# A fourth buffer for the high parts of the weights in a two-layer fp32 trunk

## What is computed

```python
def swiglu(h, w_gate, w_up, w_down):
    a = jnp.einsum('bsd,df->bsf', h, w_gate)
    b = jnp.einsum('bsd,df->bsf', h, w_up)
    return jnp.einsum('bsf,fd->bsd', jax.nn.silu(a) * b, w_down)

def moe_swiglu(h, router, w_gate, w_up, w_down):
    logits = jnp.einsum('bsd,de->bse', h, router).astype(jnp.float32)
    vals, idx = lax.top_k(logits, TOP_K)
    gates = jax.nn.softmax(vals, axis=-1)
    combine = jnp.sum(jax.nn.one_hot(idx, N_EXPERTS, dtype=jnp.float32) * gates[..., None], axis=-2)
    y = jnp.zeros_like(h)
    for e in range(N_EXPERTS):
        y = y + combine[..., e:e + 1].astype(h.dtype) * swiglu(h, w_gate[e], w_up[e], w_down[e])
    return y

# trunk, for each layer i (D_FF = 3584)
#   h = h + mixer(rmsnorm(h, norm_mix[i]), ...)
#   h = h + (swiglu if i % 2 == 0 else moe_swiglu)(rmsnorm(h, norm_ffn[i]), ...)
```

## Time and profile before

| | |
|---|---|
| three runs | 1437.06, 1436.88, 1436.52 us, median 1436.88 |
| the profiled execution | 1437.3 us, span 1435.5 us |
| PE busy (matmuls) | 1386.6 us, 97% |
| DVE busy | 1125.5 us, 78% |
| ACT busy | 966.8 us, 67% |
| granted TensorE clock, mean | 0.998 |
| memory read | 431.60 MB, 301 GB/s over the span |

### The profile page before, as it was taken

The page is one execution under the profiler, slowest core; times in us unless marked ns, Lnnn a source line. Parts: engine busy times, 40 slices in busy tenths (PEclk is TensorE's granted clock), DMA queues, the critical chain, the costliest instruction groups (busy, mean ns, idle before and its releaser), DMA issues.

```text
span 1435.5 us, 18808 instructions
## 1 busy us (share of the span) xinstructions
PE 1386.6 (97%) x6673; PEld 1089.5 (76%) x6673; DVE 1125.5 (78%) x970; ACT 966.8 (67%) x904; POOL 13.7 (1%) x26
## 2 busy tenths in 40 slices
PE   9999999999999999999999999999999999999996
PEld 7888888888788787777787777778777778777774
DVE  6575544544656699999998899998999999999997
ACT  6555434344545578788777777887788777777876
POOL 1100000000000000000000000000000000000000
PEclk9999999999999999999999999999999999999999
DMA  9813555555450099999999999999999999999993
GB/s 357 306 58 132 205 177 192 187 177 194 157 174 2 17 385 395 395 393 393 400 354 348 394 393 392 394 382 337 380 387 393 394 399 350 358 388 393 394 396 147
DMA packets 184148, 433.19 MB, mean 302 GB/s; under 512 B 7066, under 2 KB 8265, under 8 KB 184112
## 3 DMA queue, kind: packets, MB, share of 16 engines
q1 hardware_dynamic: 182064, 426.80, 81.0%
q0 software_dynamic: 1888, 5.78, 1.3%
q10 hardware_dynamic: 160, 0.14, 0.0%
HBM read 431.60 MB, written 1.09 MB: 301 GB/s over the span
## 4 chain that ended last, share of the span: by engine, by line
PE 76%; DVE 11%; issue 8%; ACT 5%; DVEq 0%; ACTq 0%
PE ps L1419 19%; PE ps L1421 19%; PE ps L1420 19%; DVE wlo L878 9%; ACT whi L514 4%; PE ps L1853 3%; PE ps L1825 2%; PE ps L1826 2%; PE ps L1548 1%; PE ps L1750 1%; PE ps L1521 1%; PE ps L1426 1%; PE ps L1814 1%; PE ps L1815 1%; PE ps L1787 1%
## 5 line engine op out<-in xcount | busy, mean ns | idle before, releaser
L878 DVE TENSOR_TENSOR wlo<-raw,whi 128x2048 fp32r<-128x2048 f32 (+1 forms) x403 | 912.7, 2286 | 210.9 <-ACT whi L514 208.3
L514 ACT ACTIVATE whi<-raw 128x2048 fp32r<-128x2048 f32 (+1 forms) x403 | 766.8, 1913 | 221.5 <-PE ps L1421 207.7
L1419 PE MATMUL ps<-whi,xhi 128*128 128x512 f32 (+1 forms) x880 | 346.0, 393 | 4.9 <-DVE wlo L878 2.4
L1421 PE MATMUL ps<-whi,xlo 128*128 128x512 f32 (+1 forms) x880 | 342.3, 389 | 0.0
L1420 PE MATMUL ps<-wlo,xhi 128*128 128x512 f32 (+1 forms) x880 | 341.7, 388 | 0.0
L1419 PEld LDWEIGHTS ps<-whi,xhi 128*128 128x128 f32 x880 | 165.3, 188 | 42.3 <-DVE wlo L878 5.8
L1421 PEld LDWEIGHTS ps<-whi,xlo 128*128 128x128 f32 x880 | 165.2, 188 | 34.4
L1420 PEld LDWEIGHTS ps<-wlo,xhi 128*128 128x128 f32 x880 | 165.3, 188 | 32.6
L1814 PE MATMUL ps<-whi,xhi 128*128 128x512 f32 x392 | 159.2, 406 | 7.0 <-DVE wlo L878 4.8
L1815 PE MATMUL ps<-wlo,xhi 128*64 128x512 f32 x392 | 154.3, 394 | 0.0
L1419 PE MATMUL ps<-whi,thi 128*128 128x512 f32 x320 | 127.3, 398 | 0.0
(11 more groups left out here) (248 smaller groups left out, 1083.5 us busy)
## 6 DMA issues: line engine op xcount, KB each, us to landing
raw<-in_moe_up SPq DMA_DIRECT2D x112, 1024.0 KB, 8.2
raw<-in_moe_gate SPq DMA_DIRECT2D x112, 1024.0 KB, 8.4
raw<-in_moe_down SPq DMA_DIRECT2D x112, 1024.0 KB, 8.4
raw<-in_ffn_up SPq DMA_DIRECT2D x14, 1024.0 KB, 5.1
raw<-in_ffn_gate SPq DMA_DIRECT2D x14, 1024.0 KB, 5.1
raw<-in_ffn_down SPq DMA_DIRECT2D x14, 1024.0 KB, 4.8
raw<-in_dil_w_in SPq DMA_DIRECT2D x10, 1024.0 KB, 5.1
raw<-in_swa_w_in SPq DMA_DIRECT2D x4, 1024.0 KB, 17.8
```

Source lines behind the costliest of these rows:

```text
L514: act.activation(whi[:, c % CUT, 0:span(c)], raw[:, c % RAW, 0:span(c)], ACT.Copy).then_inc(hi_ready, 1)
L878: dve.tensor_tensor(wlo[:, c % CUT, 0:n], raw[:, c % RAW, 0:n], whi[:, c % CUT, 0:n].bitcast(F32), ALU.subtract).then_inc(lo_ready, 1)
L1419: pe.matmul(dst, ahi, bhi, start=start, stop=False)
L1421: return pe.matmul(dst, alo, bhi, start=False, stop=stop)
```

## The change

1. `whi` has four slots (`HIS = 4`), `wlo` still three (`LOS = 3`). ACT's cut waits for the unit four before. DVE's cut gets its own wait for PE, for the unit three before. PE reads `whi[:, c % HIS]` and `wlo[:, c % LOS]`.
2. To make room, `qk` and `probsT` (attention) get places that are later those of `xhi` and `xlo`, `yhi_b` and `ylo_b` (the small expert's result) the place of `memkv`, and `stats` shrinks from 304 to 272 columns.
3. Since 6 is no multiple of 4, the dense loop now has two steps in a turn on ACT, DVE and PE: three double turns on PE; two double turns and two steps written out behind the loop on ACT and DVE.
4. In `experts`, ACT and DVE have some small steps at another place among the cuts.

```diff
-CUT = 3
+HIS = 4
+LOS = 3
@@ tiles
-        whi = sb("whi", [P, CUT, UNIT], F32R)
-        wlo = sb("wlo", [P, CUT, UNIT], F32R)
+        whi = sb("whi", [P, HIS, UNIT], F32R)
+        wlo = sb("wlo", [P, LOS, UNIT], F32R)
...
-        memkv = sb("memkv", [P, 2, TILES, 512])
+        with ExitStack() as until_routing:
+            memkv = sb("memkv", [P, 2, TILES, 512], scope=until_routing)
+        yhi_b = sb("yhi_b", [P, D], F32R)
+        ylo_b = sb("ylo_b", [P, D], F32R)
@@ cut on ACT
-                wait(act, units_done, c + RAW * rounds - CUT + 1)
-                act.activation(whi[:, c % CUT, 0:span(c)], raw[:, c % RAW, 0:span(c)], ACT.Copy).then_inc(hi_ready, 1)
+                wait(act, units_done, c + RAW * rounds - HIS + 1)
+                act.activation(whi[:, c % HIS, 0:span(c)], raw[:, c % RAW, 0:span(c)], ACT.Copy).then_inc(hi_ready, 1)
@@ dense_step on ACT (DVE alike)
-            with act.Fori(1, STEPS - 1) as s:
-                dense_step(s)
-            dense_step(STEPS - 1, True)
+            with act.Fori(0, (STEPS - 2) // 2) as k:
+                for odd in (1, 0):
+                    dense_step(2 * k + (2 - odd), odd)
+            dense_step(STEPS - 2, 1)
+            dense_step(STEPS - 1, 0, True)
@@ cut on DVE
                 dve.wait_ge(hi_ready, c + RAW * rounds + 1)
+
+                wait(dve, units_done, c + RAW * rounds - LOS + 1)
                 n = span(c)
-                dve.tensor_tensor(wlo[:, c % CUT, 0:n], raw[:, c % RAW, 0:n], whi[:, c % CUT, 0:n].bitcast(F32),
+                dve.tensor_tensor(wlo[:, c % LOS, 0:n], raw[:, c % RAW, 0:n], whi[:, c % HIS, 0:n].bitcast(F32),
                                   ALU.subtract).then_inc(lo_ready, 1)
@@ dense loop on PE
-            with pe.Fori(1, STEPS) as s:
-                products_in(FFN0 - 2, s, TILES, s * TILES)
-                unit_out(FFN0 + 2, s, dense, 0)
-                for t in range(TILES):
-                    hidden_t(t, s * TILES + t)
-                unit_out(FFN0 + 3, s, dense, 1)
+            with pe.Fori(0, STEPS // 2) as k:
+                for odd in (1, 0):
+                    s, c, even = 2 * k + (2 - odd), FFN0 + 6 * odd, 2 * k + (2 - 2 * odd)
+                    products_in(c - 2, even, TILES, s * TILES)
+                    unit_out(c + 2, even, dense, 0)
+                    for t in range(TILES):
+                        hidden_t(t, s * TILES + t)
+                    unit_out(c + 3, even, dense, 1)
```

More of the change, by code:

```diff
@@ L208, in trunk @@
             ylo = sb("ylo", [P, D], F32R, scope=glu)
-            yhi_b = sb("yhi_b", [P, D], F32R, scope=glu)
-            ylo_b = sb("ylo_b", [P, D], F32R, scope=glu)
             zero = sb("zero", [P, 512], F32R, scope=glu)
@@ L679, in _, with dense_step @@
                 glu_thi(t, t, FFN0 + 4, turned(t)[0])
-            def dense_step(s, last=False):
+            def dense_step(s, odd, last=False):
                 for i in range(4):
-                    cut(FFN0 + i, s)
+                    cut(FFN0 + 6 * odd + i, s - odd)
                 glu_silu(0, s * TILES, g_done, s + 1, rstd[:, 4:5])
@@ L686, in dense_step @@
                 for i in range(2):
-                    cut(FFN0 + 4 + i, s)
+                    cut(FFN0 + 6 * odd + 4 + i, s - odd)
                 for t in range(TILES):
@@ L798, in experts @@
                         y_hi(1, b)
-                for i in range(3, 6):
+                for i in range(3, 7):
                     cut(MOE0 + i, r)
                 large_silu(pair, 0, pair_unit(pair, 3))
-                for i in range(6, 8):
+                for i in range(7, 9):
                     cut(MOE0 + i, r)
@@ L806, in experts @@
                 put_out(pair)
-                cut(MOE0 + 8, r)
+                cut(MOE0 + 9, r)
                 sums_of(1, pair_unit(pair, 7))
-                cut(MOE0 + 9, r)
                 with act.Fori(1, STEPS) as s:
@@ L1362, in experts @@
                     c, rs = MOE0 - 4, r + 2 * s
-                    for i in range(2):
+                    for i in range(3):
                         cut(c + i, rs)
                     small_mul(pair, s - 1)
-                    for i in range(2, 5):
+                    for i in range(3, 5):
                         cut(c + i, rs)
                     small_tlo(pair, s - 1)
-                    cut(c + 5, rs)
+                    for i in range(5, 7):
+                        cut(c + i, rs)
                     large_mul(pair, s)
-                    for i in range(6, 11):
+                    for i in range(7, 11):
                         cut(c + i, rs)
@@ L1376, in experts @@
                     build_pick(pair + 1)
-                for i in range(2):
+                for i in range(3):
                     cut(MOE0 + PAIR_UNITS - 4 + i, r)
                 small_mul(pair, STEPS - 1)
-                for i in range(2):
-                    cut(MOE0 + PAIR_UNITS - 2 + i, r)
+                cut(MOE0 + PAIR_UNITS - 1, r)
                 small_tlo(pair, STEPS - 1)
@@ L1475, in chunk @@
                         last = three(dst, xhi[:, kt, t * P:(t + 1) * P], xlo[:, kt, t * P:(t + 1) * P],
-                                     whi[:, u % CUT, cols], wlo[:, u % CUT, cols], kt == 0, kt == 4 * n_units - 1)
+                                     whi[:, u % HIS, cols], wlo[:, u % LOS, cols], kt == 0, kt == 4 * n_units - 1)
                     if t == TILES - 1:
@@ L1560, in in_tile @@
                     last = three(ps[:, bank[t], :], xhi[:, kt, rows_], xlo[:, kt, rows_],
-                                 whi[:, c % CUT, cols], wlo[:, c % CUT, cols], kt == 0, kt == KT - 1)
+                                 whi[:, c % HIS, cols], wlo[:, c % LOS, cols], kt == 0, kt == KT - 1)
                 return last
@@ L1580, in out_tile @@
                         cols = slice(j * D + b * 512, j * D + b * 512 + 512)
-                        last = three(ps[:, B_Y[t][b], :], hi[:, ft, :], lo[:, ft, :], whi[:, c % CUT, cols],
-                                     wlo[:, c % CUT, cols], False, final and half == 1 and j == 1)
+                        last = three(ps[:, B_Y[t][b], :], hi[:, ft, :], lo[:, ft, :], whi[:, c % HIS, cols],
+                                     wlo[:, c % LOS, cols], False, final and half == 1 and j == 1)
                 return last
@@ L1716, in _ @@
                         last = three(ps[:, chunk_bank(c, t), :], xhi[:, kt, t * P:(t + 1) * P],
-                                     xlo[:, kt, t * P:(t + 1) * P], whi[:, u % CUT, cols], wlo[:, u % CUT, cols],
+                                     xlo[:, kt, t * P:(t + 1) * P], whi[:, u % HIS, cols], wlo[:, u % LOS, cols],
                                      kt == 0, kt == 3)
@@ L1811, in small_in @@
                     both, own = xhi[:, kt, P:2 * P], xhi[:, kt, P:P + HALF]
-                    hi, lo = whi[:, c % CUT, cols], wlo[:, c % CUT, cols]
+                    hi, lo = whi[:, c % HIS, cols], wlo[:, c % LOS, cols]
                     if kt < KT - 1:
@@ L1824, in small_products @@
                 cols = slice(j * D + b * 512, j * D + b * 512 + 512)
-                pe.matmul(ps[0:HALF, B_Y[1][b], :], thi[:, ft, P:P + HALF], wlo[:, c % CUT, cols], start=False, stop=False)
-                return pe.matmul(ps[:, B_Y[1][b], :], thi[:, ft, P:2 * P], whi[:, c % CUT, cols], start=False, stop=stop)
+                pe.matmul(ps[0:HALF, B_Y[1][b], :], thi[:, ft, P:P + HALF], wlo[:, c % LOS, cols], start=False, stop=False)
+                return pe.matmul(ps[:, B_Y[1][b], :], thi[:, ft, P:2 * P], whi[:, c % HIS, cols], start=False, stop=stop)
             def small_out(c, rounds, half, final=False):
```

37 lines of the change are left out of this document (21 added, 16 removed).

## The result

The changed kernel takes 1415.84 us (median of four runs, 1414.31 to 1417.08) against 1436.82 us for the kernel before (four runs): 21.0 us less, a ratio of 0.985 with a 95% interval of 0.9837 to 0.9862. Forecast was 19.5 us less.

The account below looks back on a forecast made before the run. The prediction took buffers and the load queue's 394 GB/s ceiling to bound expert turns equally, at 31.9 us. Gains of 16.2 + 1.3 + 2.0 = 19.5 us gave 1417.4 us, range 1409 to 1427 us (80%).

Parts of the forecast that it names:

- The bound: Expert stage: three buffers bind the 31.90 us turn, and its 12 loads at 394 GB/s take the same 31.9 us.
- Rival A: Expert stage: 394 GB/s is no ceiling, all turns fall to 30.1 us, 46 to 50 us won; chance 4%.
- B: Changes of pair: six raw buffers, freed by DVE, alone set the queue's idle time; 0 to 10 us won; chance 11%.
- The changes of pair: Three passages between expert pairs: loads run ahead there, winning 5.4 of 7.9 us idle time each, 16.2 us.
- PE's own pace: Expert turns without the limit of loads: matmuls, fold, transposes and 0.2 for passages make 30.1 us a turn.
- The first pair: Six turns before 718 us, already at the loads' ceiling: only a lead of 1.7 us to give, 1.3 taken.
- The end: Last unit of the expert stage: rounded earlier with a buffer free, 2.0 us won, bounds 0 and 2.3.
- DVE's new wait: DVE's cuts: waiting for PE directly adds no time; a fulfilled second wait costs under 0.05 us.
- Rival C: Expert loop: two semaphore tests per cut make DVE the bound; at 0.3 us each +16 us, 1453 us; chance 5%.
- The doubled dense loop: Dense loop unrolled twice: PE branches over a longer body at no cost; upper end 5.1 us, twice.
- Rival D: Dense loop: the longer body stalls PE at its branches, 5.1 us at most twice, 1422 to 1428 us; chance 4%.
- The new places: Moved qk, probsT, yhi_b, ylo_b and smaller stats: addresses only, no instruction or wait, put at nothing.

Follow-up runs that it names:

- e5: Kernel before with every load of the expert stage halved to 512 KB: 1437.74 us, ratio 1.0004.
- e8: Changed kernel with one more load of 256 KB in each of the 24 inner turns: 1430.35 us.
- e10: Changed kernel with stats back at 304 columns, so thi lies 128 bytes behind a multiple of 4096: 1417.65 us, ratio 0.9859.
- e11: Changed kernel with stats at 288 columns, so thi lies 64 bytes behind a multiple of 4096: 1416.95 us, ratio 0.9854.
- e12: Changed kernel with gate (8 bytes per partition) allocated behind both_halves instead of ahead of it: 1414.31 us, ratio 0.984.
- e3: Changed kernel with three whi buffers and the old order of small steps in experts: 1434.18 us, ratio 0.9975.
- e9: Kernel before with stats at 272 columns instead of 304, nothing else: 1433.8 us, ratio 0.9969.
- e1: Changed kernel with experts on ACT and DVE in the old order of small steps, four whi buffers kept: 1424.75 us, ratio 0.991.
- e6: Changed kernel with every load of the expert stage halved to 512 KB: 1385.32 us, ratio 0.9635.
- e7: Kernel before with one more load of 256 KB in each of the 24 inner turns: 1440.59 us, ratio 1.0016.

## Why the prediction was right, point by point

**The bound: right.** Both halves hold. Buffers bound the kernel before (e5: 31.92 us a turn with half the loads), and the loads are a ceiling at nearly the same 31.9 (late turns of the changed kernel, 394 GB/s; e8 at 32.60 with 256 KB more, 394 GB/s again). Hence the gain is not 1.8 us in each turn. Rival A is out (its own terms add up to 50 to 51 us, not to the 46 to 50 that it names), and so is B, as the stretches of 224.77 to 227.34 us show.

**The changes of pair, 16.2 us: right, 16.5 measured**, but not evenly: 231.61 became 227.34, 231.26 became 225.57, 231.30 became 224.77, that is 4.3, 5.7 and 6.5 us instead of 5.4 each. Over the 223.6 us of a stretch's loads there remain 3.7, 2.0 and 1.2 us, on the mean 2.3, where 2.4 to 2.5 were forecast. They do not lie where the forecast put them. Behind the first change the queue moves 380 GB/s in the long turn and 368 in the turn behind it, which against 394 are about 1.4 and 2.0 us of idle time; the forecast had 1.8 and 0.6. The first change gives least in e10 and e11 too; what holds it back was not tried.

**PE's own pace: 30.1 forecast, 29.86 measured.** 0.17 of it is the place of thi and tlo (e10: 30.03), the rest the allowance for passages between matmuls, which was too large. The lead is gone in two turns, or three in the last pair, where three or four were forecast. The faster pace explains only a part of that, since 6.1 us of lead at 2.0 us a turn would last three turns. The other part is probably that the queue stands idle in the turn behind the change too, and so builds less lead.

**The first pair, 1.3 us: 3.2 measured, but the lead gave what was forecast.** The forecast let the shrinking lead give 1.7 us and took 1.3. The rest comes from loads that land earlier, which the forecast did not have. This shows when one and the same load, the 51st of the expert stage, is followed through the profiled executions, together with the mark that ends the first pair (us from the start of the span):

| | 51st load lands | first pair ends | earlier than before, beyond the load |
|---|---|---|---|
| kernel before | 630.08 | 718.29 | |
| changed kernel | 628.52 | 715.13 | 1.6 |
| e10 | 630.50 | 717.12 | 1.6 |
| e11 | 629.42 | 716.02 | 1.6 |
| e12 | 628.54 | 715.16 | 1.6 |

All four have the new buffer and order, and each ends the pair 1.6 us earlier than its loads alone would make it: this is the lead, close to the 1.7 us. The other 1.6 us of the changed kernel are its loads' earlier landing, and that changes with the place of the tiles: with stats at 272 columns (changed kernel, e12) the loads land 1.5 to 1.6 us earlier than before, with 304 or 288 columns (e10, e11) 0.4 later to 0.7 earlier. The time from issue to landing is no measure of the gain. It rose by 3.0 us, from 8.4 to 11.4, and it is 11.4 in e10 too, whose first pair ends only 1.2 us earlier than before.

**The end, 2.0: right, 2.1.**

**DVE's new wait, nothing: right.** Its cuts take 2.28 to 2.29 us as before, back to back they start 2.20 us apart as before, and e3, which has the wait, is within 0.4 us of e9, which has not. Rival C is out.

**The doubled dense loop, nothing: right.** The line of the loop's branch on PE in the changed kernel, against the earlier trace rows:

```profile
L1687 PEldq COMPARE_BRANCH  x3: 76/213/226, 221.7 to 355.9; - x3
```

Starts of matmuls in the loop are nowhere more than 0.33 us apart, so no turn stalls, and e3 with the doubled loop is as fast as e9 without. Rival D is out. The Trainium skill (Runtime: NRT & Kernel Launch, Instruction fetch mechanics) has a taken branch stall when its target is not in the window of pages; no such stall is seen here. Whether the target of this branch, 304 matmuls and as many weight loads back, lies outside that window no run shows, so the trace speaks against the stall here and not against the rule.

**The new places, "at nothing, because they are addresses only": wrong.** It is the one step that failed in kind. stats at 272 columns takes 3.7 us off the kernel before (e9), and one to three us of what the changed kernel gains are its doing (e10 to e12). It does not show in PE's sums: PE was 198.00 of 198.00 us busy at either distance, since a modelled duration of 0.39 us overlaps the next start 0.23 us later. The changed kernel shows the same full sum for the dense loop, 160 to 358 us:

```profile
sum 198.00, PE 198.00 PEld 164.43 DVE 99.25 ACT 83.17 POOL 0.00; mean PE 198.00 PEld 164.43 DVE 99.25 ACT 83.17 POOL 0.00
```

Mean durations on the page of the kernel before do show it, if one asks why the same shape takes 5 to 7 ns longer with another stationary operand:

```profile
L1419 PE MATMUL ps<-whi,xhi 128*128 128x512 f32 (+1 forms) x880 | 346.0, 393 | 4.9 <-DVE wlo L878 2.4
...
L1420 PE MATMUL ps<-wlo,xhi 128*128 128x512 f32 (+1 forms) x880 | 341.7, 388 | 0.0
...
L1419 PE MATMUL ps<-whi,thi 128*128 128x512 f32 x320 | 127.3, 398 | 0.0
...
L1420 PE MATMUL ps<-wlo,thi 128*128 128x512 f32 x320 | 126.3, 395 | 0.0
```

In the dense loop the shorter distance is worth 7 steps x 48 matmuls x 5.5 ns = 1.8 us, and the first load behind routing was issued at 498.58 us instead of 501.09. Over all profiled executions that load is issued at 498.5 to 500.0 us where stats has 272 columns (nine kernels) and at 500.6 to 501.5 where it has 304 or 288 (five). None of it is left at the first mark (526.98 against 526.90). Busy time by stretch ahead of it, the kernel before, then the changed one:

```profile
425.00:500.00 75.00, 69.99 (x475) 59.17 (x474) 48.19 (x154) 40.51 (x99) 1.44 (x2) 1.00 0.03 9
500.00:530.00 30.00, 30.00 (x163) 24.75 (x163) 27.59 (x39) 20.35 (x20) 0.00 (x0) 1.00 0.96 355
```

```profile
425.00:500.00 75.00, 70.00 (x473) 59.60 (x473) 49.17 (x156) 39.10 (x99) 1.44 (x2) 0.98 0.04 9
500.00:530.00 30.00, 30.00 (x152) 24.94 (x152) 26.31 (x36) 21.53 (x20) 0.00 (x0) 0.95 1.03 381
```

The granted clock was 0.98 and then 0.95 where it had been 1.00, so for a small part of both stretches PE ran at 1.2 GHz; PE had been busy 70.0 of the 75 us ahead, in both kernels. That fits the loss, but it was not tested by a run of its own. The earlier loads were not lost: they are 1.6 of the first pair's 3.2 us.

**The total** was met because its large term, the changes of pair, was right in sum. The 2.2 us that the spans gained beyond the forecast (21.7 against 19.5) are for the most part the earlier loads of the first pair, 1.6 us, that is, the term put at nothing. That 16.2 us came out as 16.5 although the idle time lay elsewhere and the three changes differ by up to 2.2 us is partly luck.

## What to carry to other kernels

When two limits lie at nearly the same time (here buffers at 31.90 us and loads at 31.9), the waits show only one of them; divide the bytes of a turn by the best sustained rate before counting a removed wait as a gain, and look for the stretches where the second limit has slack, for there the gain will land. A little speed below the limit (0.4 us a turn in e1) is already enough to use a part of such slack. Taking half of the bytes away from both kernels (e5, e6) tells in two runs whether the other limit binds. Compare the distance between the starts of matmuls, not their busy time, and where a tile's place changes by some bytes, count that as an edit of its own.

## What the runs showed of the hardware that was not expected

- The place of a stationary operand in memory changes matmul spacing: 227 ns with thi at a multiple of 4096 bytes per partition, 232 to 233 ns with it 64 or 128 bytes further (before, e9, e10, e11), at full clock and for the same shapes. The small job's down matmuls, which read the same tile, showed no such effect (before, e9), nor did the fold, neither with its stationary operand moved by 128 bytes (e9) nor with its moving operand moved by 8 (e12).
- Over whole turns the load queue has an end at 394 GB/s: 31.9 us for 12 loads, 32.6 us with 256 KB more, in the old kernel and in the new. It is a mean. While loads are queued, one of up or gate weights lands 2.71 us after the one before it and one of down weights 2.56 us (before, changed kernel); eight and four of them are 31.9 us. The last turn ahead of a change of pair reads 399 to 401 GB/s in both kernels.
- Time from issue to landing tells whether the queue is behind: 11.4 us with six buffers when ACT waits for nearly every load, 5.1 to 5.6 us at the least around a change of pair. It does not tell how much time is to be won (e10).
- In e3, e7 and e9 the granted clock was 0.72 over 6 us near the end, in the kernel before 1.00 at the same place, after the same idle time of PE of about 2 us. The stretch behind the last mark took 24.5 to 24.6 us in these three and 23.0 in the kernel before.
